# RWKV core of a hybrid decoder trunk: the inverse is multiplied into b and A_rb, flips move to a ring of three banks, products use four places, the bonus is added ahead of the turn, and the order is new

## The chip, the cores and the metric

The kernel runs on one core of one Trainium2 chip. The metric is device time in microseconds, from runs of the whole program; three runs of the kernel before took 2577.10, 2584.65 and 2585.39 us, median 2584.65.

## The reference

Input x is 512 tokens of width 1024, float32. The trunk is: half-step SwiGLU, RWKV-7 time mixing, half-step SwiGLU, shared K/V, half-step SwiGLU, dilated attention, half-step SwiGLU. The change lies in time mixing, whose core is, for each of 16 heads of width 64:

```python
def step(S, inp):                       # S is 64x64 per head, 512 steps
    r_t, w_t, k_t, v_t, a_t, b_t = inp
    sa = jnp.einsum('bhij,bhj->bhi', S, a_t)
    S = S * w_t[:, :, None, :] + sa[..., None] * b_t[:, :, None, :] + v_t[..., None] * k_t[:, :, None, :]
    y = jnp.einsum('bhij,bhj->bhi', S, r_t)
    return S, y
...
mean = jnp.mean(y, axis=-1, keepdims=True)
var = jnp.mean(jnp.square(y - mean), axis=-1, keepdims=True)
y = ((y - mean) * lax.rsqrt(var + GN_EPS)).reshape(Bsz, T, C) * ln_w + ln_b
bonus = jnp.sum(rh * kh * r_k, axis=-1, keepdims=True) * vh
y = y.astype(h.dtype) + bonus.reshape(Bsz, T, C)
return (y * g) @ w_o, v_first
```

The kernel computes the recurrence by chunks of 64 tokens. With decay folded into the operands, each chunk needs (I - A_ab)^-1 of a strictly triangular 64x64 matrix, where A_ab = a b^T masked, and A_rb, A_ak, A_rk of the same kind. Then z = A_ak v + a S, u = inverse z, y = A_rk v + r S + A_rb u, and the next state is decay (S + k^T v + b^T u).

## The kernel before, in words

Two heads are a pair q (8 pairs), one head on partitions 0 to 63 and the other on 64 to 127; 8 chunks c per pair. A 64x64 product therefore stands on one of four places of TensorE's array: rows of one head or the other, columns 0 to 63 or 64 to 127. Each product in the code shows in the trace as two records with two weight loads.

The order of everything in the core is written out by hand in ORDER (line 32): a step such as `lift+1.2` means, in turn i of the loop, step lift of pair i+1 with number 2. `rwkv_steps` (line 50) unrolls it, and each engine runs, in this order, those steps that it has a function for. An engine waits only at semaphores, and its queue is in order, so the relative position of steps of two engines is set by the waits, not by the list.

Steps of one pair: `zwza`, `kkp` (products with two or one 512-column results: decay and learning rate; norms of kk). Scans, products by VectorE and GpSimd give ar (a and r) and bk (b and k). `ub`, `uk` (`unit_products`, L1240): 16 records each of 64x128 into a working bank; the two heads alternate, which takes two of four places. `amb`, `amk` mask them into `units`. `btp`, `ktp` (L1275, L1284) turn b and k by products with an identity, 32 records each, again on two places; ScalarE copies the result. `bsp` (L1225) gives the bonus's row sums.

The inverse is built in six levels, block size 1 to 32, on banks 2 and 3. At level l: `lift` (L1323) multiplies A by the even columns of inv_x; `gs` masks it (L1340, VectorE); `join` (L1371) multiplies with the turned inverse inv_u; `xs` adds to inv_x (L1384, VectorE); `flip` (L1353) turns inv_x again and `inv` (L1361, L1363, ScalarE) copies it to inv_u. Lift, join and flip share the two banks, so a lift waits for the copy of the flip before it. Level 0 also adds an identity (`xs` 0, L1380, VectorE). Records of lift from level 1 on, join and flip alternate over all four places.

The recurrence of chunk c: `z` (L1428, L1432) reads the state; `zs` (L1442, ScalarE) copies z; `u` (L1457) multiplies by the inverse; `us` (L1474, ScalarE) copies; `s` (L1481, L1487) updates state and y; `state` (L1502, VectorE) writes the next state with `decay` (L1446, ScalarE). Products with v (L1395, L1402, L1409) stand in `open`, `u` and `s`, one chunk at a time.

After the last chunk: `yt` copies y, `ysum`, `ycen`, `ysq`, `yvar`, `root`, `ynorm` normalise it (L1540 the last), `ytp` (L1555) turns it, `ys` scales by ln_w and adds ln_b, `bv` (L1546, GpSimd) makes the bonus, `bvp` (L1555) turns it, `ysb` (L1576) adds it, `gp` (L1580), `yg` gate it, `yhi`, `ylo` split it for the output projection. Its w_o rows are split by `split_hi` (L313, ScalarE) and `split_lo` (L318, GpSimd); four of them fall among the last pair's chunks. Two first rows of the projection (`wop`) are multiplied after the last chunk, ahead of the last pair's turn.

Results that wait for a reader (units, turns, row sums, gate and so on, 13 per pair) alternate between working banks 0 and 1: `work_free` waits until the result before it in the same bank has been read. y stands in banks 5 and 7 by turns, z and u in 4, state update in 6.

Of the kernel before, what the change touches and what calls it, by code (L numbers as in the profile page):

```python
# [21 lines left out]
P = 128  # L22
# [10 lines left out]
    open+0.0 gs+0.5 yhi-2.0 amb+1.0 ub+1.1 join+0.5 xs+0.5 uk+1.0 yt-1.0 amb+1.1 flip+0.5 amk+1.0 uk+1.1 inv+0.5  # L33
    u+0.0 lift+1.0 odd+1.0 ysum-1.0 ycen-1.0 us+0.0 s+0.0 ktp+1.0 state+0.0 gs+1.0 decay+0.1 z+0.1 xs+1.0 zs+0.1
    ktok+1.0 amk+1.1 u+0.1 flip+1.0 s+0.1 us+0.1 inv+1.0 state+0.1 lift+1.1 z+0.2 ysq-1.0 zs+0.2 zwza+2.0 decay+0.2
    u+0.2 gs+1.1 join+1.1 yvar-1.0 us+0.2 xs+1.1 tw+2.0 s+0.2 flip+1.1 state+0.2 pscan+2.0 dec+2.0 decay+0.3 z+0.3
    kkp+2.0 zs+0.3 inv+1.1 pscan+2.1 u+0.3 ta+2.0 lift+1.2 s+0.3 kk+2.0 us+0.3 undec+2.0 gs+1.2 tk+2.0 state+0.3
    join+1.2 ara+2.0 decay+0.4 z+0.4 btp+1.0 xs+1.2 zs+0.4 kp+2.0 btok+1.0 u+0.4 kka+2.0 flip+1.2 us+0.4 s+0.4
    inv+1.2 root-1.0 state+0.4 zs+0.5 rk+2.0 lift+1.3 arr+2.0 decay+0.5 z+0.5 pend+2.0 u+0.5 gs+1.3 ynorm-1.0
    uscan+2.0 us+0.5 join+1.3 s+0.5 ytp-1.0 state+0.5 uscan+2.1 z+0.6 xs+1.3 bsp+2.0 flip+1.3 ys-1.0 bvp-1.0 inv+1.3  # L40
    zs+0.6 lift+1.4 us+0.6 u+0.6 bs+2.0 s+0.6 bkb+2.0 gs+1.4 decay+0.6 ysb-1.0 state+0.6 join+1.4 bkk+2.0 z+0.7
    gp-1.0 xs+1.4 zs+0.7 u+0.7 flip+1.4 bv+0.0 us+0.7 yg-1.0 ylo-1.0 s+0.7 ub+2.0 inv+1.4 zs+1.0 lift+1.5
# [7 lines left out]
def rwkv_steps(pairs, chunks):  # L50
# [12 lines left out]
    for k in range(SLOTS):  # L63
        steps.insert(steps.index(("us", pairs - 1, k + 1)) + 1, ("wohi", pairs - 1, k))
# [4 lines left out]
    steps[steps.index(("ylo", pairs - 1, 0))] = ("ylast", pairs - 1, 0)  # L69
# [3 lines left out]
def build(nc, a, out, lo=0, upto=99):  # L73
# [13 lines left out]
    with ctx:  # L87
# [18 lines left out]
        C2_GAP = K_SQ_AT - 2 * NC * 2 * CH - (5 * T + 4 * NC * (CH + 1) + 5 * CH + 40 + 4 * NC + 4 * NC * CH + 4 * 256 + 2 * P + NC * CH)  # L106
# [6 lines left out]
        with ExitStack() as c:  # L113
            units, bk, inv_x = tensors(
                c, units=((2, 2, NC, 2 * CH), F32), bk=((2, NC, 2, CH), F32), inv_x=((2, 256), F32))
# [10 lines left out]
        with ExitStack() as c:  # L126
# [4 lines left out]
            with ExitStack() as c2:  # L131
                (tw, ta, dec, undec, resets, pcum, yt, ysq, ys, state, decayed, zs, us, cst, bs, btok, ktok, inv_u, inv_g, bv,
# [3 lines left out]
                    state=((2, CH), F32), decayed=((CH,), F32), zs=((CH,), F32), us=((CH,), F32), cst=((5, 8), F32),  # L136
                    bs=((4, NC), F32), btok=((2, NC, CH), F32), ktok=((2, NC, CH), F32), inv_u=((2, 2, 256), F32),
                    inv_g=((2, P), F32), bv=((NC, CH), F32), c2_gap=((C2_GAP,), F32), ar=((3, NC, 2, CH), F32),
# [55 lines left out]
        def col(name, k):  # L194
# [26 lines left out]
        work_read = [sem(f"work_read{i}") for i in range(2)]  # L221
# [3 lines left out]
            x_odd=1, lift=6, gs=6, join=5, xs=6, flip=6, inv=6,  # L225
            zv=NC, yv=NC, kv=NC - 1, z=NC - 1, zs=NC, u=NC, us=NC, read_out=NC - 1, st=NC - 1, decayed=NC - 2,
            state=NC - 1, y=NC, yt=1, gn=6, ysq=1, root=1, bv=1, y_hi=1, y_lo=1)
# [585 lines left out]
        def rwkv_load(sp, ph):  # L813
# [10 lines left out]
            for i, w in enumerate([1, 0, 2]):  # L824
                for k in range(0 if i else LEAD, KT):
                    load_chunk(sp, c0 + i * KT + k, row_halves(a["rwkv_w_rkv"][0, w, k * P:(k + 1) * P, :]))
            for k in range(KT):
                load_chunk(sp, c0 + 3 * KT + k, row_halves(a["rwkv_w_o"][0, k * P:(k + 1) * P, :]))

        inorms = lora_u[0:2 * KT, 1, :]  # L830

# [6 lines left out]
        def norms_act(act):  # L838
            act.wait_ge(norm_summed, 1)
            act.activation(inorms, bank[0][0:2 * KT, :], ACT.Sqrt).then_inc(norm_root, 1)  # L840
# [143 lines left out]
        def rwkv_project_pe(pe, ph):  # L984
# [52 lines left out]
            for k in range(3, KT):  # L1037
# [4 lines left out]
        WORK = dict(zwza=["zw", "za"], kkp=["kk"], bsp=["bs"], ub=["ub"], uk=["uk"], btp=["btok"], ktp=["ktok"],  # L1042
                    ytp=["yt"], bvp=["bv"], gp=["gate"])
        work_order = [(0, "zw"), (0, "za"), (0, "kk")]
        for kind, q, n in steps:
            work_order += [(q, f"{w}{n}" if kind in ("ub", "uk") else w) for w in WORK.get(kind, [])]
        work_at = {w: i for i, w in enumerate(work_order)}

        def work_bank(q, w):
            return bank[work_at[q, w] % 2]  # L1050

        def work_free(pe, q, w):

            n = work_at[q, w]
            if n >= 2:
                pe.wait_ge(work_read[n % 2], n // 2)
# [5 lines left out]
        def read_work(ins, q, w):  # L1062
            ins.then_inc(work_read[work_at[q, w] % 2], 1)

        def after_read(eng, q, w):

            if q >= 0:
                n = work_at[q, w]
                eng.wait_ge(work_read[n % 2], n // 2 + 1)
# [19 lines left out]
        def blocks(t, l, e):  # L1089

            return t.rearrange("p v (k e r) -> p v k e r", e=2, r=1 << l)[:, :, :, e, :]

        def lev(l, n):

            return psum[:, 2:4, 0:n].rearrange("p v (k r) -> p v k r", r=1 << l)

        def am_b(q):
            return units[:, 1 - q % 2, 0]

        def am_k(q):  # L1100
            return units[:, 1 - q % 2, 1]
# [1414 lines left out]
```

## Time and profile before

| | |
|---|---|
| median of three runs | 2584.65 us (2577.10 to 2585.39) |
| profiled execution: span (its time beyond the span is not given) | 2577.7 us |
| TensorE busy | 2504.1 us, 97% |
| VectorE, ScalarE, GpSimd busy | 33%, 37%, 38% |
| the core's seven full turns | 229.7 us, TensorE busy 202.28 |

The profiled execution's own time is its span, 2577.7 us, and what lies around it, which the page does not give; the span is 6.95 us below the median of the runs. The core takes roughly 546 to 831 us of the span. Windows are cut where `open` of a pair starts. Busy time of TensorE counts a record from start to modelled end, and records on different places overlap, so the pace of a group is read from the starts or from the merged rows of weight loads. The granted clock is 1.00 at 2.4 GHz and 0.50 at 1.2 GHz; a mean in between is a mixture of the two.

### The profile page before, as it was taken

To read this page: it belongs to the slowest core of one execution; us is meant where nothing else is said; L and a number is where in the kernel's file an instruction comes from. 1 tells how busy PE (TensorE), PEld (TensorE's weight loads), DVE (VectorE), ACT (ScalarE), POOL (GpSimd) and SP (SyncE) were. 2 spreads that over 40 slices of the span, in tenths; PEclk is the share of its full clock that TensorE was granted. 3 is DMA by queue.
4 is the path that set the end of the run, shared out by engine and by line. 5 is a ranking of instruction groups with operands and counts; after the bars stand their busy time and mean duration, and the time that the engine had idled before them with its cause. 6 is when DMAs were issued, how large, how long until landed. Compare 5 with 4: busy or idle time off the path is not lost.

```text
span 2577.7 us, 46700 instructions
## 1 busy us (share of the span) xinstructions
PE 2504.1 (97%) x18778; PEld 2053.7 (80%) x18794; DVE 859.3 (33%) x1300; ACT 953.4 (37%) x1572; POOL 991.0 (38%) x470
## 2 busy tenths in 40 slices
PE   8999999999888999999999999999999998999998
PEld 6888877777776788888888888888888777788887
DVE  5222036455554332210433122221054567322200
ACT  4233225534543343321443333332153565333321
POOL 4444453322222354444443444444454101444442
PEclk9999999988988999999999999999999999999999
DMA  4333222210000233322243443333232241333321
GB/s 153 95 97 98 98 82 98 74 34 4 4 4 25 77 107 97 98 98 98 94 152 123 142 144 98 98 98 98 95 110 90 66 127 55 98 98 98 98 96 59
DMA packets 181773, 230.37 MB, mean 89 GB/s; under 512 B 16408, under 2 KB 119992, under 8 KB 181624
## 3 DMA queue, kind: packets, MB, share of 16 engines
q1 hardware_dynamic: 181624, 228.20, 27.9%
q8 instruction: 115, 1.88, 0.3%
q14 instruction: 34, 0.28, 0.0%
HBM read 213.47 MB, written 14.68 MB: 89 GB/s over the span
## 4 chain that ended last, share of the span: by engine, by line
PE 83%; issue 11%; POOL 2%; DVE 2%; ACT 2%; DMA 0%; SPq 0%; POOLq 0%; ACTq 0%; DVEq 0%
PE bank L343 19%; PE bank L345 19%; PE bank L344 19%; PE bank L350 5%; PE bank L352 5%; PE bank L351 5%; POOL w_lo L318 2%; PE bank L1353 1%; PE bank L1240 1%; PE bank L1323 1%; PE bank L1371 1%; PE bank L990 1%; PE bank L1823 1%; DVE xg_lo L1803 1%; PE bank L1555 1%
## 5 line engine op out<-in xcount | busy, mean ns | idle before, releaser
L318 POOL TENSOR_TENSOR w_lo<-w_raw,w_hi 128x1024 fp32r<-128x1024 f32 x376 | 906.8, 2416 | 1309.3 <-ACT w_hi L313 1308.5
L313 ACT ACTIVATE w_hi<-w_raw 128x1024 fp32r<-128x1024 f32 x376 | 395.4, 1058 | 1008.9 <-PE bank L345 860.4
L343 PE MATMUL bank<-xg_hi,w_hi 128*128 128x512 f32 x1408 | 550.1, 391 | 5.7 <-POOL w_lo L318 3.1
L345 PE MATMUL bank<-xg_hi,w_lo 128*128 128x512 f32 x1408 | 548.6, 390 | 0.0
L344 PE MATMUL bank<-xg_lo,w_hi 128*128 128x512 f32 x1408 | 548.5, 390 | 0.0
L343 PEld LDWEIGHTS bank<-xg_hi,w_hi 128*128 128x128 f32 x1408 | 264.8, 188 | 63.6 <-issue 7.6
L344 PEld LDWEIGHTS bank<-xg_lo,w_hi 128*128 128x128 f32 x1408 | 264.7, 188 | 55.7 <-issue 0.7
L345 PEld LDWEIGHTS bank<-xg_hi,w_lo 128*128 128x128 f32 x1408 | 264.7, 188 | 54.6
L343 PE MATMUL bank<-hid_hi,w_hi 128*128 (+1 forms) x704 | 274.4, 390 | 0.0
L345 PE MATMUL bank<-hid_hi,w_lo 128*128 (+1 forms) x704 | 273.9, 389 | 0.0
L344 PE MATMUL bank<-hid_lo,w_hi 128*128 (+1 forms) x704 | 273.9, 389 | 0.0
L571 DVE TENSOR_TENSOR gate<-bank,rstd 128x512 f32<-128x512 f32 x88 | 56.7, 686 | 638.2 <-PE bank L345 638.2
L350 PE MATMUL bank<-w_hi,xg_hi 128*128 128x512 f32 x576 | 226.9, 394 | 0.0
L352 PE MATMUL bank<-w_lo,xg_hi 128*128 128x512 f32 x576 | 224.4, 390 | 0.0
L351 PE MATMUL bank<-w_hi,xg_lo 128*128 128x512 f32 x576 | 224.2, 389 | 0.0
L377 DVE SCALAR_TENSOR_TENSOR x<-bank,x 128x512 f32<-128x512 f32 x48 | 32.7, 686 | 378.2 <-PE bank L345 378.1
L343 PEld LDWEIGHTS bank<-hid_hi,w_hi 128*128 128x128 f32 x704 | 132.1, 188 | 28.2 <-DVE up L577 1.1
L345 PEld LDWEIGHTS bank<-hid_hi,w_lo 128*128 128x128 f32 x704 | 132.2, 188 | 27.5
L344 PEld LDWEIGHTS bank<-hid_lo,w_hi 128*128 128x128 f32 x704 | 132.2, 188 | 27.5
L352 PEld LDWEIGHTS bank<-w_lo,xg_hi 128*128 128x128 f32 x576 | 108.1, 188 | 22.7
L351 PEld LDWEIGHTS bank<-w_hi,xg_lo 128*128 128x128 f32 x576 | 108.2, 188 | 21.8 <-issue 0.2
L350 PEld LDWEIGHTS bank<-w_hi,xg_hi 128*128 128x128 f32 x576 | 108.3, 188 | 21.5 <-issue 0.2
(290 smaller groups left out, 3142.5 us busy)
## 6 DMA issues: line engine op xcount, KB each, us to landing
w_raw<-in_ffn_w_in SPq DMA_DIRECT2D x352, 256.0 KB, 3.0
w_raw<-in_ffn_w_out SPq DMA_DIRECT2D x176, 256.0 KB, 2.7
w_raw<-in_w_kv SPq DMA_DIRECT2D x96, 256.0 KB, 3.1
w_raw<-in_rwkv_w_rkv SPq DMA_DIRECT2D x48, 256.0 KB, 2.9
w_raw<-in_attn_w_q SPq DMA_DIRECT2D x48, 256.0 KB, 3.1
k_dram<-stage SPq DMA_DIRECT2D x6, 1024.0 KB, 4.6
v_dram<-stage SPq DMA_DIRECT2D x6, 1024.0 KB, 5.5
keys<-k_dram SPq DMA_DIRECT2D x24, 256.0 KB, 3.4
```

The lines of the kernel that those rows point to most:

```text
L313: act.activation(w_hi[:, s, :], w_raw[:, s, :], ACT.Copy).then_inc(w_hi_ready, 1)
L318: pool.tensor_tensor(w_lo[:, s, :], w_raw[:, s, :], w_hi[:, s, :].bitcast(F32), ALU.subtract).then_inc(w_lo_ready, 1)
L343: pe.matmul(o, hi, x_hi, start=start, stop=False)
L344: pe.matmul(o, hi, x_lo, start=False, stop=False)
L345: return pe.matmul(o, lo, x_hi, start=False, stop=stop)
L350: pe.matmul(o, x_hi, hi, start=start, stop=False)
L351: pe.matmul(o, x_lo, hi, start=False, stop=False)
L352: return pe.matmul(o, x_hi, lo, start=False, stop=stop)
L377: dve.scalar_tensor_tensor(x[:, m], bank[m][:, :], ph["scale"], x[:, m], ALU.mult, ALU.add).then_inc(x_new, 1)
L571: dve.tensor_tensor(gate[:, f], bank[4 * half + f][:, :], rstd[:, :], ALU.mult).then_inc(gate_scaled, 1)
L990: last = pe.matmul(bank[b][:, :], w, x[:, k], start=k == 0, stop=k == KT - 1)
L1240: last = pe.matmul(work_bank(q, w)[head(hh if which == 0 else 1 - hh), c % 4 * P:(c % 4 + 1) * P], bk[head(hh), q % 2, c, which, :], ar[he ...
```

## The change

- ORDER is replaced by a new list of 120 steps; the loop's turns run over the same pairs, with up to three pairs behind (`yhi-3.0`).
- `ub`+`uk` become `un`: products for b and k alternate record by record, so that the four places are all used; `btp`+`ktp` become `tu` in the same way.
- Working banks are 0, 1, 2 instead of 0, 1. A result takes the bank used longest ago; readers count on one semaphore per reading engine. The flips of a level take two of these banks (`flip0_`, `flip1_`), and `inv` copies each with an instruction of its own. Lift and join alone use banks 3 and 4.
- Level 0 of lift also multiplies an identity with the identity (8 records of 128 columns), so that the masked result already has the diagonal; `xs` 0 and the last flip are dropped: levels of flip go from 0 to 4.
- New: `ba` multiplies the finished inverse into A_rb and b (32 records of 128 columns, two working banks), copied back by ScalarE (`baa`) and VectorE (`bad`). `s` then takes zs directly; `u`, `us` are gone.
- `open` issues the products with v of all chunks at once into banks 5 (y), 6 (z) and 7 (state update), one y bank instead of two.
- ln_w is loaded again as rows, broadcast over tokens, by two DMAs on SP's queue behind a wait for the last projection row and ahead of the w_o rows. GpSimd multiplies the normalised y by it (`weigh`) and adds the bonus (`joined`), for the last pair VectorE does both; one turn `ytp` follows. `bvp`, `ysb` are gone.
- kk's product contracts over 64 rows instead of 16, the others zero (a GpSimd memset among the weight splits).

```diff
-        def ub_pe(pe, q, n):
-            need(pe, "ar", q)
-            need(pe, "bk", q, 1)
-            unit_products(pe, q, f"ub{n}", n, 0)
+        def un_pe(pe, q, n):
+            need(pe, "ar", q)
+            need(pe, "bk", q)
+            for w in ("ub", "uk"):
+                work_free(pe, q, f"{w}{n}")
             for c in range(4 * n, 4 * n + 4):
                 for hh in range(2):
+                    for which, w in enumerate(("ub", "uk")):
+                        last = pe.matmul(work_bank(q, f"{w}{n}")[head(1 - hh if which else hh), c % 4 * P:(c % 4 + 1) * P],
+                                         bk[head(hh), q % 2, c, which, :], ar[head(hh), 2 - q % 3, c, :, :],
+                                         start=True, stop=True)
...
+        def ba_pe(pe, q, _):
+            need(pe, "xs", q)
+            for w in ("ub0", "ub1", "btok"):
+                after_read(pe, q, w)
+            for v in range(2):
+                work_free(pe, q, f"ba{v}")
+            for cc in range(4):
+                for v in range(2):
+                    for hh in range(2):
+                        c = 4 * v + cc
+                        last = pe.matmul(work_bank(q, f"ba{v}")[rows_of(c, hh), cc * P:(cc + 1) * P],
+                                         inv_x[head(hh), c * CH:(c + 1) * CH], am_b(q)[head(hh), c, CH:3 * CH],
+                                         start=True, stop=True)
...
         def flip_pe(pe, q, l):
-            need(pe, "xs", q, l + 1)
             if l == 0:
+                need(pe, "gs", q, 1)
                 need(pe, "x_odd", q)
+            else:
+                need(pe, "xs", q, l)
+            for v in range(2):
+                work_free(pe, q, f"flip{v}_{l}")
...
         def open_pe(pe, q, _):
             if q == 0:
                 values_copied(pe, 7)
-            need(pe, "us", q - 1)
-            need(pe, "yt", q - 2)
-            for n in range(2):
-                after_read(pe, q, f"uk{n}")
-            z_values(pe, q, 0)
-            y_values(pe, q, 0)
+            need(pe, "zs", q - 1)
+            need(pe, "yt", q - 1)
+            for w in ("uk0", "uk1", "ktok"):
+                after_read(pe, q, w)
+            for c in range(4):
+                last = z_values(pe, q, c)
+                y_values(pe, q, c)
+            done(last, "zv")
...
+        def weigh_pool(pool, q, _):
+            if q == 0:
+                pool.wait_ge(lora_landed, 16 * 8)
+            need(pool, "gn", q)
+            done(pool.tensor_tensor(chunks(yt[:, :]), chunks(yt[:, :]), ln_w[:, q].unsqueeze(1).to_broadcast([P, NC, CH]),
+                                    ALU.mult), "tail")
```

TensorE's part of one turn in the new order:

```
bsp+0.0 flip+0.2 s-1.3 lift+0.3 z-1.4 join+0.3 s-1.4 lift+0.4 z-1.5 flip+0.3 ytp-2.0 s-1.5 join+0.4 z-1.6
flip+0.4 s-1.6 lift+0.5 gp-2.0 z-1.7 un+1.0 s-1.7 join+0.5 un+1.1 open+0.0 ba+0.0 lift+1.0 tu+1.0 s+0.0
lift+1.1 z+0.1 flip+1.0 s+0.1 z+0.2 zwza+2.0 join+1.1 s+0.2 flip+1.1 lift+1.2 kkp+2.0 z+0.3 join+1.2
```

## Rows read from the trace of the kernel before

**Rows 1.** the page: span, busy time of each engine, the last chain by engine.

```profile
span 2577.7 us, 46700 instructions
...
PE 2504.1 (97%) x18778; PEld 2053.7 (80%) x18794; DVE 859.3 (33%) x1300; ACT 953.4 (37%) x1572; POOL 991.0 (38%) x470
...
PE 83%; issue 11%; POOL 2%; DVE 2%; ACT 2%; DMA 0%; SPq 0%; POOLq 0%; ACTq 0%; DVEq 0%
```

**Rows 2.** windows of the core: length, busy by engine, clock, DMA share, GB/s.

```profile
546.20:576.90 30.70, 25.26 (x695) 22.16 (x696) 15.26 (x28) 9.67 (x21) 5.40 (x4) 0.72 0.01 3
...
639.50:671.35 31.85, 27.92 (x1029) 23.89 (x1023) 18.81 (x39) 16.52 (x44) 8.25 (x7) 1.00 0.02 4
...
576.90:806.60 229.70, 202.28 (x7007) 175.31 (x6999) 120.27 (x257) 104.30 (x290) 50.13 (x43) 0.91 0.02 4
...
806.60:830.80 24.20, 18.51 (x378) 13.89 (x372) 8.21 (x17) 11.71 (x32) 7.01 (x4) 0.65 0.14 46
...
830.80:844.60 13.80, 11.86 (x100) 8.99 (x96) 6.15 (x7) 2.74 (x5) 6.44 (x3) 0.88 0.24 78
```

**Rows 3.** timeline, full clock: start, duration, engine, line, operation, shape, count.

```profile
640.94 0.85 PEld L1240 LDWEIGHTS bank<-ar,bk 64*64 64x64 f32 x16
...
644.88 0.90 PEld L1284 LDWEIGHTS bank<-ident,bk 64*64 64x64 f32 x28
...
648.52 0.59 PEld L1323 LDWEIGHTS bank<-inv_x,units 64*64 64x64 f32 x32 [0.65 <-issue]
...
649.30 0.69 PE L1116 MATMUL bank<-lora_u,lora 64*128 64x512 f32 x1
...
649.83 0.59 PE L1116 MATMUL bank<-lora_u,lora 64*128 64x512 f32 x1
...
650.52 0.60 PEld L1371 LDWEIGHTS bank<-inv_g,inv_u 64*64 64x64 f32 x32
```

**Rows 4.** by source line, whole span: minimum/median/maximum ns of one instruction.

```profile
L1555 PEld LDWEIGHTS bank<-ident,yt x256: 129/135/223, 629.8 to 842.4; 64*64 64x64 f32 x128
...
L1540 DVE TENSOR_TENSOR yt<-yt,cst x8: 675/692/2358, 628.8 to 836.1; 128x512 f32<-128x512 f32 x8
...
L1546 POOL TENSOR_TENSOR bv<-v,bs x8: 1042/1042/1044, 600.1 to 827.2; 128x512 f32<-128x512 f32 x8
```

**Rows 5.** chain that ended last, around pair 7: start, duration, what.

```profile
808.48 0.77 PE bank L1353 x32
...
809.70 0.37 PE bank L1457 x2
...
812.83 0.09 ACT w_hi L313
...
819.31 0.50 PE bank L1428 x4
...
820.11 0.37 PE bank L1457 x2
...
820.96 0.37 PE bank L1481 x2
...
821.82 0.51 PE bank L1428 x4
```

**Rows 6.** groups by line over the seven turns: busy us, mean ns, idle before.

```profile
L1363 ACT ACTIVATE inv_u<-bank 128x256 f32<-128x256 f32 x35 | 13.5, 387 | 25.8 <-PE bank L1353 25.7
...
L1474 ACT ACTIVATE us<-bank 128x64 f32<-128x64 f32 x56 | 12.5, 224 | 31.5 <-PE bank L1457 30.9
...
L1259 DVE TENSOR_TENSOR units<-bank,umask 128x512 f32<-128x512 f32 x28 | 18.6, 682 | 0.4 <-PE bank L1240 0.4
...
L1576 DVE TENSOR_TENSOR ys<-ys,bank 128x512 f32<-128x512 f32 x6 | 4.1, 677 | 0.0
...
L1508 ACT ACTIVATE yt<-bank 128x512 f32<-128x512 f32 x6 | 3.5, 588 | 0.0
```

**Rows 7.** DMA issues: engine, count, KB each, median us from issue to landing.

```profile
w_raw<-in_rwkv_w_o SPq DMA_DIRECT2D x16, 256.0 KB, 2.7
```

More of the change, by code:

```diff
@@ new lines, in build @@
+        READS = dict(act=dict(tw=["zw"], ta=["za"], bs=["bs"], btok=["btok"], ktok=["ktok"], baa=["ba0"], ys=["yt"],
+                              inv=["flip0_", "flip1_"]),
+                     dve=dict(kk=["kk"], amb=["ub"], amk=["uk"], bad=["ba1"], yg=["gate"]))
+        read_at = {(0, "zw"): ("act", 1), (0, "za"): ("act", 2), (0, "kk"): ("dve", 1)}
+        reads = dict(act=2, dve=1)
+        for kind, q, n in steps:
+            for engine, kinds in READS.items():
+                if kind in kinds:
+                    for w in kinds[kind]:
+                        reads[engine] += 1
+                        read_at[q, f"{w}{n}" if kind in ("amb", "amk", "inv") else w] = (engine, reads[engine])
@@ L1283, in ktp_pe @@
                 for hh in range(2):
-                    last = pe.matmul(work_bank(q, "ktok")[head(1 - hh), c * CH:(c + 1) * CH], bk[head(hh), q % 2, c, 1, :],
-                                     ident2[head(hh), :], start=True, stop=True)
-            last.then_inc(work_done, 1)
+                    for which, w in enumerate(("btok", "ktok")):
+                        last = pe.matmul(work_bank(q, w)[head(1 - hh if which else hh), c * CH:(c + 1) * CH],
+                                         bk[head(hh), q % 2, c, which, :], ident2[head(hh), :], start=True, stop=True)
+                        if c == NC - 1 and hh == 1:
+                            last.then_inc(work_done, 1)
         def btok_act(act, q, _):
@@ L1324, in lift_pe @@
+            if l == 0:
+                for v in range(2):
+                    for hh in range(2):
+                        even = blocks(ident2[head(hh), :], 0, 0).rearrange("p k r -> p (k r)")
+                        last = pe.matmul(bank[LEVEL_BANK + v][head(hh), 0:4 * 32], ident2[head(hh), :],
+                                         even.unsqueeze(1).to_broadcast([CH, 4, 32]), start=False, stop=True)
             done(last, "lift")
         def odd_pool(pool, q, _):
-            need(pool, "flip", q - 1)
@@ L1355, in flip_pe @@
-            done(last, "flip")
+            for cc in range(4):
+                for v in range(2):
+                    for hh in range(2):
+                        c = 4 * v + cc
+                        src = ident2[head(hh), :] if l == 0 else blocks(ident2[head(hh), :], l, 1)
+                        last = pe.matmul(work_bank(q, f"flip{v}_{l}")[tile_rows(v, hh), cc * n:(cc + 1) * n],
+                                         inv_x[head(hh), c * CH:(c + 1) * CH], src, start=True, stop=True)
+                    if cc == 3:
+                        last.then_inc(work_done, 1)
@@ L1394, in z_values @@
             for hh in range(2):
[L1395 to L1397 removed]
+                last = pe.matmul(bank[6][rows_of(c, hh), c * CH:(c + 1) * CH], am_k(q)[head(1 - hh), c, 0:CH],
+                                 v2[head(1 - hh), q, c, :], start=c == 0, stop=True, skip_group_check=True)
+            return last
@@ L1684, in rwkv_pool @@
                     need(pool, "y", q - 1)
+                    need(pool, "join", q)
                     split_lo(pool, ph["c0"] + 3 * KT + n)
```

425 lines of the change are left out of this document (225 added, 200 removed).

## Prediction, on record before the changed kernel ran

> **What bounds the kernel now.** I read the page's head first: TensorE is busy for 97% of a span of 2577.7 us, and the chain that ended last is TensorE for 83% [rows 1]. The change touches the RWKV core alone, so the next view is busy time by window. From the first unit product (546.2 us) to the start of pair 7's recurrence (806.6) and its last turned chunk (830.8), the core takes 284.6 us. In its seven full turns of the loop (229.7 us) TensorE is busy 88%, VectorE 52%, ScalarE 45%, GpSimd 22% [rows 2]; DMA moves 4 GB/s, so no transfer matters here. TensorE's order decides, and the reader should split it in two: records at their own pace, and time waiting for another engine's hop.
>
> The pace is in the rows of weight loads at the full clock [rows 3]. Each product in the code shows as two records. Where two places of the array alternate, 16 records of 128 columns take 0.85 us (53 ns each), 28 of 64 columns take 0.90, which less the last load's own 0.14 [rows 4] is 28 ns each. Where all four places alternate, 32 records of the inverse (64x32) take 0.60 us, 14.8 ns each. Records of 512 columns start 0.53 us apart, a group of two 1.06. One turn, 639.5 to 671.35, ran wholly at the granted clock 1.00 (the 2.4 GHz level) in 31.85 us [rows 2]. Its content: units 64 x 53 = 3.4 us; six two-place groups of 32 (two turns of b and k, y, bonus, row sums, level-0 lift) 6 x 0.90 = 5.4; sixteen four-place groups (lift, join, flip) 16 x 0.47 = 7.6; 244 records of the recurrence at some 18 ns = 4.4; tw/ta, kk and gate 3.2. Sum 24.0, so 7.8 us are waiting. Both chains show such waits: recurrence z, zs, u, us, s, state, and inverse flip, copy, lift, mask, join, add, flip [rows 5].
>
> **Part by part, one turn at full clock.**
> Units and turns on four places: an instruction takes its place's time, whoever stands next to it, so pace per record halves for 128 columns: 64 x 26.5 = 1.7, minus 1.7 us. For 64 columns four places are bounded by 28/2 = 14 ns and the measured 14.8: the two turns take 64 x 14.8 = 0.95 instead of 1.8, minus 0.85. If alternation bought nothing both stay, which is the other bound (0).
> The Trainium skill ("TensorE: Matmul & The Clock Gate", section "Wait — 56ns, not 53.3ns?") says start-to-start never falls below about 25 ns. By that the turns would take 1.6 us and gain only 0.2. The trace disagrees on four places (0.59 us for 32 loads, 18 ns even with the last one's length [rows 3]), so I leave the sum.
> Bonus added ahead: its turn (0.90) and VectorE's add (0.68 [rows 6]) go; GpSimd gets a multiplication and an add. A GpSimd product of this size takes 1.04 us [rows 4]; I take 2 x 1.2 for both, on an engine busy 22%. Only y's turn waits for them, a turn later, so 0.
> The Trainium skill ("SBUF — State Buffer", section "🔬 SBUF: two separate sides") lets a VectorE op with two SBUF inputs and a reading GpSimd op exclude each other. The normalisation, an op of that kind, took 675 to 2358 ns [rows 4]; these rows don't say what stretched the longest. Two more GpSimd ops could cost one such collision per turn, up to 1.7 us on VectorE; most would be hidden, and this is inside my range.
> Inverse folded in: the product u (32 records, 0.6) and copies us (8 x 0.22 on ScalarE [rows 6]) go; `ba` adds 32 four-place records of 128 columns (0.85), one copy of half on each of ScalarE and VectorE (0.59 and 0.68, as 128x512 reads of a bank [rows 6]). Level 0 takes its identity on TensorE: 8 records of 128 columns on two places, plus 0.42; VectorE loses one add.
> Flips in the ring: `ba` makes the last level's flip needless, so 32 records (0.47) go. The five left have their copies cut in two; ScalarE pays some 0.15 more on each. Bound: 0 to 5 x 0.39 us [rows 6] there; ScalarE has 15 us free. A flip now overlaps the lift instead of standing between join and lift.
> Opening all eight value products at once: same records, all four places, 0. `open` on one y bank must wait for yt of the previous pair. Behind it TensorE has ba, the next lift and turns. A join and a unit group (0.5 + 0.85) stand between and cover ScalarE's 0.59 copy [rows 6]; without cover 0.9 x 7 = 6 us.
> Padding kk's contraction from 16 to 64 rows, two broadcasts of ln_w, GpSimd's memset: 0. The loads wait in SP's queue for the last projection row, and the 16 w_o half-loads queue behind them; but w_o is first split at 812.8 us [rows 5], over 250 us later, and the first use of ln_w is a turn away. If a needed load were late it costs about its landing once, 2.7 us for w_o's [rows 7].
> Net pace: 24.0 - 1.7 - 0.85 - 0.9 - 0.6 - 0.47 + 0.85 + 0.42 = 20.8 us.
>
> Waiting: before, TensorE meets another engine's hop at about 40 places per turn (8 u, 8 s, 7 z, and 17 between groups of the inverse): 7.8/40 = 0.195 us each. After, u's eight and the flips' six are off the chain: 26 places, 5.1 us. I add 0.3 for the three-bank ring. Turn 20.8 + 5.4 = 26.2, minus 5.65. The mean turn before is 32.8 because part ran at the lower level (mean clock 0.91 [rows 2]); I keep the saving, **7 x 5.65 = 39.6 us**. That assumes the same clock. Both ends: -3.2 x 7 if no wait goes, -8.5 x 7 if they fall to 2.5.
>
> Fill (546.2 to 576.9): the inverse of pair 0 runs almost bare. Flip and copy take 808.48 to 809.70 = 1.22 us per level [rows 5], six levels 7.3, units 1.7 less, level-0 and ba 1.3 more: minus 7.7, and 0.3 for more than half of it at the 1.2 GHz level (0.72): **-8**.
> Drain (806.6 to 830.8): a bare chunk is 819.31 to 821.82 = 2.51 us, of which u and us are 820.11 to 820.96 = 0.85 [rows 5]. Seven chunks 6.0, less 1 for w_o splits and pair 6's tail, which still stand among them: **-5**.
> Last pair's tail (830.8 to 844.6): on VectorE a multiplication, 0.69 or, as the longest normalisation, up to 2.36 [rows 4], and an add stand ahead of its turn; a turn and an add go behind it. Bounds -1 to +3, nearest **+0.5**: w_o rows run meanwhile.
> Sum -52.1: span 2577.7 to 2525.6. Only the span of the profiled execution is given; the three runs are 2577.1 to 2585.39, so it lies at their low end, 6.95 below their median. From the median, 2584.65 - 52.1 = **2532.5 us**.
>
> **Rivals.**
> A. The waits stay. In-order queues and ring waits keep 7.8 us a turn; only pace goes: 7 x 3.2 = 22, fill 4, drain 2: about 2557. For it: each wait goes to whoever is late next, and VectorE carries 18.8 us of the 31.85. Against: 14 hops are really gone from both chains.
> B. Waits collapse: turn 23.5: 7 x 8.3 = 58, plus 12: 2514. For it: bare chains are 8 x 1.66 = 13 and about 14 us, both far under 20.8. Against: one in-order queue interleaves both.
> C. The ring turns the sign. Now 13 results per turn share two banks: 31.85 x 2/13 = 4.9 us per stay, though product, hop and read are only 0.85 + 0.68 plus little. Afterwards 24 results share three banks (10 are flips, two at once). From a mean stay of 31.85 x 3/24 = 4.0 us the turn is longer than now; at 4.5 it is 36, 7 x 4.15 - 12 = +17: 2602. The needed stay of some 1.8 says 14.4 us, no bound; a read queued behind other work says otherwise. The same banks also hold the next unit products.
> D. Clock. The lower level covers 17 us of the fill (0.72), 17 of the drain (0.65) and about 40 in the turns. A turn at half clock has 20.8 us more of pace. If its share goes from 0.18 to 0.45, 0.27 x 20.8 x 7 = +39: 2572, hardly beyond the noise. The trace shows the fall after stretches with thin records (fill, drain); TensorE's share of pace rises in my turns from 75 to 79%, against it.
> That the arithmetic doesn't do what it says is no rival that changes time.
>
> **Numbers.** Forecast (2517 to 2549) 0.47; A 0.20; B 0.12; D 0.09; C 0.08; anything else 0.04. A measurement here tells no change to about 0.3%, 7.8 us: faster means below 2577. Faster: 0.47 + 0.20 + 0.12 + half of D = 0.84; same 0.06; slower 0.10. The range goes from just below B's centre to just short of D's, 2511 to 2569; outside lie some 0.2, most above.
>
> **What would show it.** Steps right: full-clock turns of 26 to 27 us; unit and turn loads at 27 and 15 ns; no records of u and us; bare chunks of 1.6 to 1.7 us; about 26 waits per turn, longest total still on ScalarE's zs or VectorE's mask; fill about 23 us, drain 19. Wrong: unit products still at 53 ns; TensorE waiting on inverse copies or unit masks for a bank before a flip or unit group (C); granted clock below 0.85 over the turns (D); turns near 29 with VectorE's state behind normalisation and scans (A).

## The result, and the profile after

The changed kernel takes 2560.35 us (median of four runs, 2558.26 to 2564.64) against 2583.95 (2577.10 to 2585.39) for the kernel before, run beside it: ratio 0.9926, 95% interval 0.991 to 0.9941. The medians are 23.6 us apart; the interval says 15 to 23. Forecast were 52.1 less. The direction was right and the time lies in the stated range, but less than half of the gain came; the number nearest to it is that of rival A, 2557.

The page's head answers to [rows 1]:

```profile
span 2562.6 us, 45662 instructions
...
PE 2479.9 (97%) x18346; PEld 2025.3 (79%) x18346; DVE 867.9 (34%) x1294; ACT 946.5 (37%) x1550; POOL 1011.4 (39%) x485
...
PE 81%; issue 13%; POOL 3%; DVE 2%; ACT 1%; DMA 0%; SPq 0%; POOLq 0%; ACTq 0%; DVEq 0%
```

TensorE lost 24.2 us of busy time and 432 products; the span lost 15.1. In the last chain TensorE's share fell by two points and "issue" rose by two: time in which it waited for nothing that the profile shows.

The windows answer to [rows 2] (same columns): fill; its stretch at the lower clock; the seven turns; two turns at full clock; the drain with the 1.3 us behind it.

```profile
546.00:582.50 36.50, 29.86 (x750) 25.38 (x754) 16.13 (x31) 9.71 (x24) 3.58 (x3) 0.58 0.23 67
...
551.30:582.10 30.80, 27.37 (x674) 23.33 (x677) 11.79 (x22) 8.28 (x20) 3.58 (x3) 0.50 0.15 55
...
582.50:792.40 209.90, 178.08 (x6628) 150.58 (x6621) 126.75 (x249) 99.36 (x273) 69.08 (x56) 0.91 0.02 4
...
638.90:667.20 28.30, 24.05 (x970) 20.18 (x964) 20.73 (x38) 15.40 (x41) 11.93 (x9) 1.00 0.02 4
...
667.20:698.20 31.00, 24.42 (x971) 20.44 (x961) 20.42 (x38) 15.31 (x41) 11.93 (x9) 1.00 0.02 4
...
792.40:815.00 22.60, 14.54 (x274) 9.97 (x274) 6.69 (x17) 10.54 (x25) 9.39 (x6) 0.60 0.15 49
```

The fill grew from 30.7 to 36.5 us, and 30.8 of them ran at granted clock 0.50, the 1.2 GHz level, where before it was 17 of 30.7. The turns at full clock take 28.3 and 31.0 us, not 26.2. The first turn, which has no `ytp` and `gp` yet, took 26.4. The mean clock over the seven turns is the same 0.91, with 37.5 us at the lower level; before it was 41.0.

The pace rows answer to [rows 3] (timeline of weight loads at full clock: start, duration, line, count):

```profile
605.59 0.89 PEld L1287 LDWEIGHTS bank<-ar,bk 64*64 64x64 f32 x32 [0.33 <-issue]
...
643.13 1.18 PEld L1316 LDWEIGHTS bank<-ident,bk 64*64 64x64 f32 x63
...
646.18 0.59 PEld L1396 LDWEIGHTS bank<-ident,inv_x 64*64 64x64 f32 x32 [1.04 <-DVE inv_g L1380]
...
670.00 0.89 PEld L1447 LDWEIGHTS bank<-units_b,inv_x 64*64 64x64 f32 x32
```

Unit products (L1287) load 32 in 0.89 us where 16 took 0.85. The turns of b and k (L1316) load 63 in 1.18, 17 ns apart once the last load's 0.13 is taken off; forecast were 15. The new group ba (L1447) takes 0.89, forecast 0.85.

Now the view that the prediction's sum of waits did not draw on: what TensorE's products waited for over the seven turns (total us, times, longest; waits over 150 ns). First the kernel before, then the one after.

```profile
PE bank L1457 <- ACT zs L1442: 4.7, 14, 0.6
PE bank L1323 <- ACT inv_u L1361: 4.1, 7, 0.6
PE bank L1353 <- issue: 2.4, 4, 1.0
PE bank L1353 <- DVE inv_x L1384: 1.9, 6, 0.3
PE bank L1481 <- ACT us L1474: 1.6, 7, 0.3
PE bank L1428 <- DVE state L1502: 0.3, 1, 0.3
```

```profile
PE bank L1515 <- DVE state L1569: 4.3, 10, 0.8
PE bank L1352 <- DVE inv_x L1430: 2.9, 7, 0.8
PE bank L1396 <- DVE inv_x L1430: 2.8, 8, 0.4
PE bank L1447 <- issue: 2.7, 3, 1.2
PE bank L1422 <- DVE inv_g L1380: 2.1, 6, 0.6
PE bank L1287 <- DVE units_b L1298: 2.1, 5, 0.5
PE bank L1396 <- ACT ktok L1329: 0.9, 1, 0.9
```

Summed, this view gives 26.2 us before and 30.8 after. Waits that end with another engine are 17.0 us (46 times) before and 16.4 (40 times) after: before, 13.1 of them end with ScalarE and 3.9 with VectorE; after, 2.2 and 14.2. Those marked issue rose from 9.2 to 14.4. What stands outside the waits went from 203.5 to 179.1.

The same view of the load queue must be read with care, since a weight load also stands still while a long product ahead of it runs. Here the load of u shows a wait for ScalarE, and the product of u shows none, for 512-column products were running:

```profile
649.83 0.59 PE L1116 MATMUL bank<-lora_u,lora 64*128 64x512 f32 x1
...
650.35 0.14 PEld L1457 LDWEIGHTS bank<-zs,inv_u 64*64 64x64 f32 x2 [0.76 <-ACT zs L1442]
...
650.35 0.27 PE L1457 MATMUL bank<-zs,inv_u 64*64 64x64 f32 x2
```

Such stretches come to 14.4 us over the turns before, nearly all put down to another engine, and to 15.7 after, all marked issue. Whoever goes by the load queue alone therefore sees waits for engines fall from 30.7 to 21.0 us, which the products did not gain.

Part of the issue time can be seen directly: pauses of over 250 ns from one product to the next of the same source line, with no semaphore between them and no 512-column product ahead. Over the turns there are 19 before, 12.3 us in all, and 22 after, 17.6 us; one more, of 2.3 us, ends at 795.91 in the opening of pair 7. Every one of these 42 ends 2.2 to 2.8 us after the start of a transfer of program code (16 KB on queue 8, one per some 256 TensorE instructions). That the transfer is what TensorE stands for is read from this, and no run changes the transfers alone. One of them, in the timeline and in the DMA view of 698 to 702 us in 40 slices:

```profile
699.66 0.88 PEld L1447 LDWEIGHTS bank<-units_b,inv_x 64*64 64x64 f32 x30
...
702.01 0.19 PEld L1447 LDWEIGHTS bank<-units_b,inv_x 64*64 64x64 f32 x2 [1.47 <-issue]
```

```profile
GB/s 0 0 0 0 0 0 0 0 0 0 0 0 164 0 0 0 0 0 0 0 0 0 0 0 0 0 0 0 0 0 0 0 0 0 0 0 0 0 0 0
...
q8 instruction: 1, 0.02, 2.1%
```

Thirty loads of one group run, the last two come 1.5 us later. The only traffic is a code transfer at 699.2, 2.8 us before they do.

The pair of profiled executions, split at the forecast's own borders:

| part | forecast | measured |
|---|---|---|
| fill, 30.7 to 36.5 us | -8 | +5.8 |
| seven turns, 229.7 to 209.9: outside the products' waits | -22.4 | -24.4 (203.5 to 179.1) |
| the same: waits | -17.2 | +4.6 (26.2 to 30.8) |
| drain, 24.2 to 21.3 | -5 | -2.9 |
| tail and rest | +0.5 | +2.1, and -0.2 ahead of the core |
| sum (span 2577.7 to 2562.6) | -52.1 | -15.1 |

The medians are 23.6 apart, since this profiled execution is the slowest of its kernel's four and that of before lies low in its own. A second profile of the changed kernel (run 17) has the products' waits at 26.1 us over the turns, 13.7 of them ended by another engine, and 68.3 us of its turns at the lower clock.

### The profile page after: what moved, and what is told of

Read it like the earlier page. It is cut to its first block, busy times and chain, and to the rows that moved or that the text cites. A ratio compares the mean times of both kernels' runs of the same rounds, so it can differ in the third digit from the quotient of the medians.

```text
span 2562.6 us, 45662 instructions
## 1 busy us (share of the span) xinstructions
PE 2479.9 (97%) x18346; PEld 2025.3 (79%) x18346; DVE 867.9 (34%) x1294; ACT 946.5 (37%) x1550; POOL 1011.4 (39%) x485
## 4 chain that ended last, share of the span: by engine, by line
PE 81%; issue 13%; POOL 3%; DVE 2%; ACT 1%; DMA 0%; SPq 0%; POOLq 0%; ACTq 0%; DVEq 0%
PE bank L346 19%; PE bank L347 19%; PE bank L348 19%; PE bank L353 5%; PE bank L355 5%; PE bank L354 5%; POOL w_lo L321 2%; PE bank L1396 1%; PE bank L999 1%; PE bank L1906 1%; PE bank L1352 1%; PE bank L1287 1%; PE bank L1422 1%; DVE xg_lo L1886 1%; PE bank L1215 0%
```

## The experiments

Each median is of one batch, its ratio is to the kernel before in the same batch. Kernels are the changed one with one edit unless said otherwise. "Lower" is the time in the turns at granted clock 0.50 in the profiled execution; the changed kernel has 37.5 us of it, and 68.3 in run 17. The intervals of these ratios are some 8 us wide, so differences of 3 to 5 us between two runs do not stand alone.

**1. Do four places pay?** Units and turns were issued as before, on two places.

```diff
-for c in ...:
-    for hh in range(2):
-        for which, w in enumerate(("ub", "uk")):
+for which, w in enumerate(("ub", "uk")):
+    for c in ...:
+        for hh in range(2):
```

> The changed kernel, but units and turns are issued first all of b, then all of k, so that two of the four places alternate, as before the change. All else is the same. If pace counts fully: a unit group of 32 records goes from about 0.92 to 1.7 us and the turns from 1.26 to 1.8, 2.1 us per pair, 17 us in all, to about 2577. If other waits take what four places gave (waits stay, whoever is late next): at most 5 us, about 2563 to 2565.

Measured: 2561.22 us (2551.41 to 2565.07), ratio 0.9906 [0.9887, 0.9925]. Its row of a unit group, to set against the 0.89 above:

```profile
637.04 1.38 PEld L1287 LDWEIGHTS bank<-ar,bk 64*64 64x64 f32 x32 [0.59 <-issue]
```

Each group of units and turns is slower, some 1.4 us a turn or 10 in all, and the time is the same. What four places save, something else takes back: in this kernel the pauses inside groups are 14, 8.3 us over the turns, against 22 and 17.6 (15 and 13.7 in run 17), and the products' waits marked issue are 6.0 us against 14.4 (12.4).

**2. Is GpSimd's tail in the way?** The two new GpSimd operations and nothing else were cut from 512 to 8 columns, for the first seven pairs; this leaves out most of ln_w and of the bonus.

```diff
-pool.tensor_tensor(yt[:, :], yt[:, :], flat(bv[:, :, :]), ALU.add)
+pool.tensor_tensor(yt[:, 0:8], yt[:, 0:8], flat(bv[:, :, :])[:, 0:8], ALU.add)
```

> The changed kernel with GpSimd's multiplication by ln_w and its bonus add cut to 8 of 512 columns for the first seven pairs: this leaves out most of ln_w and of the bonus. In the changed trace the scan ucum takes 1.10 us against 0.69 before, and the two products ar 1.13 and 1.15 against 0.68 and 0.79; over seven turns 9.8 us of VectorE. If these GpSimd operations hold VectorE up and that is on the path: scans back to 0.69 and 6 to 10 us less, about 2552. If VectorE has slack there: scans back to 0.69 but within 2 us of the changed kernel. If they don't collide: scans stay at 1.1.

2559.97 us, 0.9905 [0.9888, 0.9921]. The scan on VectorE over the turns, in the changed kernel and in this one:

```profile
L1185 DVE TENSOR_TENSOR_SCAN ucum<-undec,resets 128x260 f32<-128x260 f32 x12 | 13.2, 1099 | 0.3 <-ACT undec L1181 0.3
```

```profile
L1185 DVE TENSOR_TENSOR_SCAN ucum<-undec,resets 128x260 f32<-128x260 f32 x12 | 8.3, 688 | 0.1
```

The new operations do stretch VectorE's scan by 0.41 us each, and it costs nothing that this measurement can tell: the scans aren't on the path.

**3. Can the fill's clock be held?** Products of 128 columns into a spare bank stand among the inverse of pair 0.

```diff
+if q == 0:
+    keep_busy(pe, 7, 4)   # four 128x128 products, also after each join; two after each flip
```

> The changed kernel with 2 or 4 extra 128x128 products into unused bank 7 behind each lift, flip and join of pair 0, in the time in which TensorE waits for other engines. In the changed trace 551 to 582 us ran at clock 0.5. Clock theory: the clock stays at 1.00 for most of the fill, it takes 36.5 - 10 us, total about 2550. Rival: the fill is a chain of hops and the extra products only add their time, or the clock falls all the same: total the same or up to 5 us more.

2574.17 us, 0.9965 [0.9951, 0.9979]: 14 slower than the change, or 10 by the ratios. The clock did stay up, 0.91 in the fill, yet the fill grew:

```profile
545.60:585.40 39.80, 36.57 (x859) 31.60 (x862) 15.76 (x31) 9.78 (x24) 3.58 (x3) 0.91 0.20 62
```

The 3.3 us that the fill grew are not the whole 10 to 14, and the rest is not located. Filler put into a bare chain gained nothing: as I read it, it stands in the chain and took what the clock gave.

**4. The units alone, on the kernel before.**

```diff
-ub+1.1 ... uk+1.1     # two steps, one bank each
+un+1.1                # one step on four places, both banks
```

> The kernel before with one part of the change alone: unit products for b and k alternate record by record over four places, in two groups per pair instead of four, and the masks are moved accordingly. Pace theory: 1.6 us per pair less, 13 us in all, about 2571. Waits-stay theory: one pair of groups needs both working banks at once, so the wait for a mask takes the gain: 2578 to 2586.

2594.03 us, 1.0043 [1.0026, 1.006], 10 us slower than before. A group that takes both working banks at once needs both free. Over its seven turns TensorE's products wait 28.3 us for another engine, before it was 17.0; new in the list is the first lift of each pair, which waits for VectorE's unit masks:

```profile
PE bank L1337 <- DVE units L1273: 4.6, 7, 0.7
```

The change has a third bank, and its unit groups still wait for the masks, 2.1 us over the turns.

**5 to 8. What does TensorE's time cost, and what a hop?** Four edits, each a known amount of work with a result that is overwritten.

```diff
+pe.matmul(work_bank(q, "btok")[:, :], lora2[...], lora_u[...])      # few_long: one of 512 columns a pair, 1.06 us
+for ...: pe.matmul(work_bank(q, w)[...], bk[...], ident2[...])       # many_short: the 32 turns twice
+again(act, lambda: act.activation(scratch, bank[6][...], ACT.Copy))  # zs twice, seven pairs
+again(dve, lambda: dve.tensor_tensor(scratch, src, mask, ALU.mult))  # the inverse's mask twice
```

> The changed kernel with one extra product of 512 columns ahead of each pair's turns: two records, 1.06 us of TensorE per pair at full clock, 8.5 us in all. Waits-stay theory (TensorE's pace has slack, as undoing the four places cost nothing): 0 to 3 us more, at most 2564. Pace theory: 8 to 10 us more, about 2569.

2556.94 us, 0.9897 [0.9882, 0.9911]: 8.5 us of work more, and 3 us less time (four runs; the intervals of the two ratios just overlap). Mean clock 0.984 to 0.988, lower 10.2.

> The changed kernel with the turns of b and k issued twice: 64 more records and 64 more weight loads per pair, about 1.15 us of TensorE at the measured pace, nearly the time of the two long records of the other kernel but 32 times their instructions. If code loading holds TensorE up (in the trace, pauses of 1.0 to 1.5 us inside a group end 2.2 to 2.8 us after an instruction transfer has started): more than e5 by half a transfer's pause per pair, 4 us or more. If not: the same as e5 within 2 us.

2586.99 us, 1.0014 [1.0, 1.0028]: 27 us more than the change for 8 us of array time. Lower 96 us, mean clock 0.973.

> The changed kernel with ScalarE's copy zs made twice (once to scratch) for seven pairs: 56 times 0.22 us and a short wait in the recurrence's chain, 13 to 15 us if the recurrence decides. If the inverse decides, or TensorE's pace: under 5 us.

2564.73 us, 0.992 [0.9905, 0.9934]. 12 to 15 us added to the recurrence cost some 4, which is within the noise.

> The changed kernel with VectorE's mask of each level from 1 on made twice (once to scratch): 40 times 0.42 us and a short wait in the inverse's chain and in VectorE's queue, 17 to 19 us if the inverse's chain or VectorE's queue decides. If the recurrence alone decides: the mask stands between its state updates too, 3 to 8 us.

2566.07 us, 0.9928 [0.9915, 0.9941]. 17 us (40 times 0.42) added to the inverse cost some 6, hardly beyond it. So neither chain alone is the bound, and the one long product a pair costs nothing.

**9. Fewer records.** The row sums' 32 records became one product of 512 columns, so the row sums are left out.

```diff
-for c in range(NC):
-    for hh in range(2): last = pe.matmul(work_bank(q, "bs")[head(1 - hh), c:c + 1], ...)
+pe.matmul(work_bank(q, "bs")[:, :], lora2[...], lora_u[...])
```

> The changed kernel with the 32 records of the bonus's row sums replaced by one product of 512 columns (2 records, 1.06 us instead of 0.7; the row sums are wrong, so the bonus is). 60 of some 1890 TensorE instructions per pair go, its time rises by 0.35 us. Instruction theory (a 16 KB code transfer of 256 instructions every 3.85 us at full clock sets the turn): 60/256 x 3.85 = 0.9 us per pair, 7 us less, about 2553. Pace theory: 3 us more.

2564.28 us, 0.9949 [0.9932, 0.9965]. Its four ordinary turns at full clock are 27.8, 28.1, 28.5 and 29.5 us, a little short; but 61 us of its turns ran lower, and nothing was gained.

**10 and 11. The same on the kernel before:** one long product a pair, and k's turn three times.

```diff
+pe.matmul(work_bank(q, "ktok")[:, :], lora2[...], lora_u[...])       # few_long
+for c in 2 * list(range(NC)): ... pe.matmul(work_bank(q, "ktok")...)  # many_short
```

> The kernel before with one extra product of 512 columns per pair ahead of the turn of k: 2 records, 1.06 us, 8.5 us in all. If the instruction stream bounds the kernel before too (transfers 4.04 us apart at full clock): no more than 3 us above before. If its own pace does: 8 to 10 us more, about 2593.

2583.34 us, 1.0019 [1.0006, 1.0031]: some 5 us for the 8.5 added, with an interval of 1.5 to 8.

> The kernel before with the turn of k issued three times: 64 more records and 64 more loads per pair, on two places 1.5 to 1.8 us. Instruction theory: 128/256 x 4.04 = 2.0 us per pair, 16 us, and up to 27 as in e6 where the clock falls more often, 2600 to 2611. Pace with slack: nothing beyond e10 but 0.5 us per pair, 4 us.

2591.54 us, 1.0049 [1.0033, 1.0064]: 12 us for some 15 of array time (64 loads more, 1.9 us a pair). In the kernel before, added array time costs half or more of itself. So its slack was smaller than in the changed kernel, and nothing like the jump of run 6 is seen.

**12. A quarter of the records** in levels 3 and 4, each group filled up with one product of 164 columns: 264 TensorE instructions a pair fewer. It leaves out three quarters of these levels' products, so the inverse is not the true one.

```diff
+if l in (3, 4): long_instead(pe, bank[LEVEL_BANK])   # 164 columns
-for cc in range(4):
+for cc in range(4 if l not in (3, 4) else 1):
```

> The changed kernel with lift, join and flip of levels 3 and 4 cut from 32 records to 8 each, and one product of 164 columns ahead of each, so that each group takes TensorE about its old time (the inverse is wrong from level 3 on). All waits, copies, masks and adds stay. 132 fewer records and as many fewer loads per pair, 264 instructions. Instruction theory: 264/256 x 3.85 = 4.0 us per pair, 25 to 31 us less, about 2530. If the waits between engines bound the turn: 0 to 5 us less.

2582.21 us, 1.0008 [0.9995, 1.0021], 22 us slower than the change. This theory, that the count of instructions is the price, predicted some 2530 and fell. The pauses inside groups did go, from 17.6 to 8.2 us, but its turns ran at 0.80:

```profile
581.00:805.90 224.90, 203.72 (x5700) 162.37 (x5692) 124.35 (x248) 100.05 (x273) 68.01 (x56) 0.80 0.01 3
```

**13. The same count, fuller.** The fillers of 164 columns became 512; the inverse is again not the true one.

> The kernel after, with levels 3 and 4 of the inverse at a quarter of their products as in the run before it (the inverse is not the true one), and each of the four replaced groups and the flip filled by one product of 512 columns (two records, 1.06 us at full clock) instead of 164 columns: the same count of instructions, 0.7 us more of TensorE work in each group, 3.6 to 4.3 us per pair. If the clock is what kept fewer records from paying: the half-clock time in the turns falls from 95 us to below 75 and the median stays at or falls below the 2582 of the thinner one, in spite of 25 to 30 us more work. If the lower clock there was incidental and TensorE's time counts: 2582 + 25 = 2607.

2624.42 us, 1.0166 [1.0145, 1.0186]. The clock didn't come back (mean 0.961 to 0.974), and here the added array time, 25 to 30 us, cost 42. As I read it, a long product inside the inverse's chain lengthens the chain.

**14 and 15. More array time in the changed kernel.** Two long products a pair; then one long product with units and turns on two places, the edit of run 1.

```diff
+for _ in range(n):   # ahead of the second unit group; the other as in run 5
+    pe.matmul(work_bank(q, f"ub{n}")[:, :], lora2[...], lora_u[...])
```

> The kernel after, with two products of 512 columns per pair added (ahead of the turns of b and k, and ahead of the second unit group): 2.1 us more TensorE work per pair at full clock, 17 us in all, results overwritten. One such product gave 2556.9. If the array's time has slack and steady work holds the clock: 2550 to 2560, mean clock 0.984 or more. If the slack is used up by the first: 2562 to 2566. If the array's work counted in full against the change: 2577.

2563.65 us, 0.9935 [0.9917, 0.9954]: 17 us of work for 3 us of time, mean clock 0.978 to 0.986.

> The kernel after, with units and turns issued on two places (as before the change) and the one product of 512 columns per pair: 2.4 us more of array time per pair than the change, 19 us in all. Slack theory: 2552 to 2562, clock 0.984 or more. Pace theory (the forecast's own): 2577 or more.

2555.64 us, 0.9901 [0.9886, 0.9916]: 19 us of array time more than the change, and less time.

```profile
578.20:785.70 207.50, 184.60 (x6638) 154.55 (x6635) 129.47 (x249) 99.64 (x273) 70.67 (x56) 0.96 0.02 4
607.20:637.00 29.80, 26.83 (x968) 21.93 (x964) 19.55 (x39) 15.09 (x40) 10.22 (x8) 1.00 0.02 4
637.00:666.90 29.90, 26.04 (x970) 21.60 (x968) 20.78 (x39) 15.47 (x41) 11.90 (x9) 1.00 0.02 5
```

Its turns at full clock are 29.8, 29.9, 29.9 and 29.7: TensorE's busy time rose by 2 us on that of the changed kernel's turns and the turn stayed between its 28.3 and 31.0. The clock over the turns is 0.96, not 0.91.

**16. Quarter of the records, with two long products outside the inverse,** which is again not the true one.

> The kernel with levels 3 and 4 at a quarter of their products, each group filled by 164 columns (the inverse is not the true one; it took 2582 us at mean clock 0.966 to 0.972), and two products of 512 columns per pair ahead of the turns and the second unit group. If what a turn costs at full clock goes by the number of TensorE instructions (some 15.5 ns each, 264 fewer per pair), turns that run wholly at 2.4 GHz take 26 to 27.5 us, and with the clock back at 0.98 the median is 2530 to 2550. If fewer instructions buy nothing at any clock: full-clock turns of 29.5 or more and 2565 or more. If the clock doesn't come back: mean below 0.975 and 2575 to 2600.

2592.72 us, 1.0047 [1.003, 1.0064]; mean clock 0.966 to 0.973, so the clock didn't come back. One turn ran at 0.99 nevertheless:

```profile
612.60:641.50 28.90, 26.74 (x840) 20.27 (x836) 19.49 (x38) 15.08 (x40) 10.26 (x8) 0.99 0.02 4
```

It took 28.9 us, where the count of instructions asked for 26 to 27.5. Fewer instructions bought next to nothing even there.

**17 and 18. Side by side:** the changed kernel unaltered, and run 15's kernel again.

> The changed kernel unaltered, beside the next one in the same rounds, so that the two can be compared on one chip: 2558 to 2564, as before.

2563.33 us (2558.08 to 2568.09), 0.9937 [0.9922, 0.9951].

> The changed kernel with units and turns on two places and one product of 512 columns per pair, again: 2555 to 2558, 3 to 6 us below the changed kernel beside it, at a mean clock 0.984 or more. If the difference of the earlier batches was the chip's: the same as the changed kernel beside it.

2558.11 us (2557.68 to 2562.28), 0.9923 [0.991, 0.9935]. The two intervals overlap; over both batches the kernel with thicker TensorE work has eleven runs with median 2557.7, the changed one ten with median 2562.1 and none under 2558.08. That is some 4 us, on two batches; with run 5's 2556.94 (four runs) these are the fastest found.

## Why the prediction was wrong

**The saving of pace was right and didn't turn into time by itself.** TensorE is busy for 27.9 us of the full-clock turn before [rows 2] and for 24.1 and 24.4 of the two after: forecast were 3.2 less, measured 3.5 to 3.9. Single terms: units 2 x 0.9 for 1.7, ba 0.89 for 0.85; the turns of b and k 1.08 to 1.38, where no longer pause falls into them, instead of 0.95. Beside the row of the turns stands the rule of the Trainium skill that the prediction weighed ("TensorE: Matmul & The Clock Gate", section "Wait — 56ns, not 53.3ns?"), a floor of some 25 ns from start to start: this row's 17 ns is under it, as the rows before were.

**The failed step is "Waiting: 7.8/40 = 0.195 us each ... After ... 26 places, 5.1 us".** It has two faults. The 7.8 us were what a sum of groups (24.0) left of the turn. But that turn has TensorE busy for 27.92 of 31.85 us [rows 2], so 3.9 us idle: by that account, which counts a record up to its modelled end, half of the 7.8 was no waiting at all. And the waiting was shared out over 40 hops and taken to go with each hop removed. The products' view has 46 waits for another engine over all seven turns, 6.6 a turn, and 40 after. The waits of u and s for ScalarE's copies and of the lifts for the inverse copy are gone (L1457, L1481 and L1323 above, and 1.6 us more of L1323: 12.0 us), and the sum is still 16.4 for 17.0. In its place z waits for VectorE's state (4.3 for 0.3), lifts and flips for VectorE's add (5.7 for 1.9), and unit groups and one flip for a bank of the ring (3.0 for nothing). The second profile has 13.7 us for 17.0, 11.6 of it on VectorE. A wait moved on to whoever came late next; it didn't go with its hop.

This is rival A, the waits stay, with its number, 2557, and in good part with its argument: the longest wait in the list is now z on VectorE's state. Not among A's grounds was the growth of the waits marked issue, 9.2 to 14.4 us (12.4 in run 17). With it go the pauses that end behind a code transfer. In nine profiles with four places (two of the changed kernel, and runs 2, 3, 5, 7, 8, 9 and 14) they sum to 12.0 to 19.7 us over the turns, in the three with two places (runs 1, 15, 18) to 5.8 to 9.2. So most of what run 1 gave up in pace it got back there. That faster records make TensorE run ahead of its code is my reading of it; the kernel before has two places too, and 12.3 us.

**Fill: -8 came out as +5.8.** Two things. The clock: 30.8 us at the lower level instead of 17. In the second profile of the changed kernel (run 17) the fill ran at 0.78 and took 30.5 us:

```profile
546.20:576.70 30.50, 23.23 (x751) 20.29 (x754) 16.74 (x31) 9.67 (x24) 3.59 (x3) 0.78 0.25 80
```

So some 6 of the 14 us are clock. The other 8 are in the row too, for at a clock like that of before the fill still gained nothing. In this profile level 1 to level 5 took 16.7 us instead of 21.3, so the flips did leave the chain (-4.6). But from the first unit product to level 1 it is 9.3 instead of 7.6: the second unit group, which needs two banks of three, stands for 2.3 us until VectorE's masks have read one.

```profile
PE bank L1287 <- DVE units_b L1298: 2.3, 1, 2.3
```

And from the lift of level 5 to the first `s` it is 9.4 instead of 5.8, for two unit groups of the next pair, the eight openings and ba now stand there. (The table's border, the first opening, falls into this stretch: it lies 4.6 us into it, before it was 1.0. Up to the first `s` it is 35.4 us before and in run 17.) I had given level 0 and ba 1.3 us together and the openings nothing, since in the turns they have cover; in the fill they have none.

**Drain: right in its core.** From the first to the last chunk of pair 7 it is 15.3 us against 20.1, 4.8 less for a forecast of 5, and a bare chunk takes 1.67 us against 2.51 (z of chunk 2 at 800.85, of chunk 3 at 802.52). Ahead of it the opening and ba took back some 2; the pause of 2.3 us that ends at 795.91 falls there. First z of a bare chunk, then its s, at the lower clock:

```profile
800.85 0.18 PEld L1515 LDWEIGHTS bank<-state,ar 64*64 64x64 f32 x2 [0.56 <-DVE state L1569]
...
801.65 0.18 PEld L1547 LDWEIGHTS bank<-zs,units_b 64*64 64x64 f32 x2 [0.50 <-ACT zs L1531]
```

**Clock (rival D): half right.** It was rejected with "TensorE's share of pace rises". Its busy share at full clock did not: 27.92 of 31.85 us before (88%), 24.05 of 28.3 (85%) and 24.42 of 31.0 (79%) after. Of the turns 41.0 of 229.7 us ran lower before, 37.5 of 209.9 after, but 68.3 of 215.3 in run 17, a share of 0.32 for the 0.45 that D feared. Within one kernel time goes with mean granted clock: over 126 runs of the changed kernel and all the experiments, each batch about its own mean, 1.5 us per 0.001, correlation -0.91. In the batch of run 17 the kernel before has 0.9825 and the changed one 0.9783, worth 6.5 us. The direction of the rest agrees: runs 5, 15 and 18, with a long product added, have 0.9855 to 0.987 and take 3 to 5 us less, run 14 with two of them 0.9825 and takes no less; with thinner records it is 0.965 to 0.969. That the clock is the cause of these and not a mark of something else is not shown; in run 3 it was held up and time was lost.

**Rivals B and C.** The waits didn't collapse. C's sign, TensorE waiting on unit masks for a bank, is there at a small size: 2.1 us in five waits over the turns (3.0 in six in run 17) and 2.3 in the fill. The 1.04 us ahead of a flip [shown above, 646.18] are of that kind too. The load queue puts them down to VectorE's mask, but that mask was done; the products' view names ScalarE's copy of the turn of k, whose bank the flip took. With 0.9 us for that the ring costs 3.0 us over the turns, for the 7 x 0.3 = 2.1 forecast. Run 4 shows the mechanism on two banks: 10 us.

**VectorE and GpSimd.** The scan went from 0.69 to 1.10 us beside GpSimd and back without it. The Trainium skill ("SBUF — State Buffer", section "🔬 SBUF: two separate sides") has the two engines exclude each other on such operations; these rows agree in kind. The forecast hid it at nothing, and run 2 bears that out.

**What stays open.** After the change an ordinary turn at full clock takes 28 to 31 us, and it still does with 2.4 us more of TensorE work or with 14% fewer TensorE instructions, and 2 us more in either chain costs about a third of itself, hardly beyond the noise. No single one of these sets the turn; which schedule of the two chains would, wasn't tried, since the order could be changed only as a whole.

## What to carry to other kernels

Before pricing a removed hop, read how long the bottleneck engine's products really wait, and what ended each wait. What a sum of groups leaves over is not waiting, and the load queue of TensorE also stands behind long products. Then ask who comes late next: of 17.0 us of waits for other engines 12.0 belonged to hops that were removed, and 16.4 remained. Test the slack first: add a known amount of work and see what it costs, since time that can be added for nothing can be removed only for nothing. And count in the fill and the drain each group that has cover in the loop, because there it has none.

## What the runs showed that I had not expected

- Adding work made the kernel faster: one 512-column product a pair with units and turns on two places, 19 us of TensorE time, took 4 to 5 us off.
- The same added time costs by its grain and place: 8.5 us in long products -3 us, 8 us in short records +27, 25 to 30 us of long products inside the inverse's chain (13 against 12) 42 us.
- Code is fetched 16 KB at a time, 55 times in the turns before and 52 after, one per some 256 TensorE instructions, at full clock on average 3.9 to 4.0 us apart and in these two profiles never less than 3.3. A pause in a group ended 2.2 to 2.8 us after a fetch had begun, in all 42 cases.
- The waits for other engines changed their owner and hardly their sum: before, 13.1 of 17.0 us ended with ScalarE, after, 14.2 of 16.4 with VectorE.
- Thinning the inverse's records to a quarter dropped the mean clock from 0.980 to 0.968 and cost 22 us although 264 instructions a pair were gone.
